# Two-layer decoder trunk: the dense SwiGLU stage with gate and up weights side by side and products of 512 columns

## The reference

```python
def swiglu(h, w_gate, w_up, w_down):
    return (jax.nn.silu(h @ w_gate) * (h @ w_up)) @ w_down

h = rmsnorm(x, ffn_norm[0])                  # 256 x 1024
x = x + swiglu(h, dense_w_gate[0], dense_w_up[0], dense_w_down[0])   # 1024 x 2816, 2816 x 1024
```

## Time and profile before

| what | value |
|---|---|
| time, median of 3 runs | 1540.76 us (1540.14 to 1541.29) |
| time of the profiled execution | 1540.58 us |
| its span | 1538.7 us |
| TensorE busy | 1500.0 us, 97% |
| VectorE busy | 1201.2 us, 78% |
| ScalarE busy | 965.0 us, 63% |
| dense stage, first product to the first instruction behind it | 316.33 to 512.81 us of the span |
| mean granted TensorE clock, share of full | 0.992 |

### The profile page before, as it was taken

One profiled execution on the slowest core, in us unless ns is written; L12 is line 12 of the kernel. 1 busy time (PEld: TensorE's weight loads), 2 busy tenths in 40 slices (PEclk: granted clock), 3 DMA queues, 4 the chain that ended last, 5 costly groups with the idle time before them and its releaser, 6 DMA issues.

```text
span 1538.7 us, 21907 instructions
## 1 busy us (share of the span) xinstructions
PE 1500.0 (97%) x8346; PEld 1286.5 (84%) x8346; DVE 1201.2 (78%) x986; ACT 965.0 (63%) x801; POOL 113.8 (7%) x64
## 2 busy tenths in 40 slices
PE   6999999999999989999999999999999999999996
PEld 6999999889998868888888888888888888888885
DVE  7877677664445678888888888888888888888886
ACT  4444444454343657777777777777777777777775
POOL 1332232100000000000000000000000000000000
PEclk9999999999999999999999999999999999999999
DMA  9644334265456388999999899899899999999980
GB/s 376 211 137 138 138 137 138 85 197 188 169 191 247 137 328 342 378 357 399 353 363 404 341 367 400 349 354 403 347 377 380 359 369 376 364 378 359 395 324 29
DMA packets 66862, 449.40 MB, mean 292 GB/s; under 512 B 7648, under 2 KB 9440, under 8 KB 14448
## 3 DMA queue, kind: packets, MB, share of 16 engines
q1 hardware_dynamic: 63264, 439.84, 74.2%
q0 software_dynamic: 3392, 8.69, 2.2%
q10 hardware_dynamic: 144, 0.02, 0.0%
HBM read 440.65 MB, written 7.86 MB: 291 GB/s over the span
## 4 chain that ended last, share of the span: by engine, by line
PE 93%; DVE 3%; DMA 1%; ACT 1%; issue 1%; SPq 0%; DVEq 0%; ACTq 0%
PE bank L376 29%; PE bank L377 29%; PE bank L378 29%; PE bank L1360 2%; PE bank L1513 2%; DVE w_lo L328 1%; DMA raw<-in_units 1%; PE bank L1347 1%; PE bank L1337 1%; DVE rot L890 1%; PE bank L1522 0%; ACT w_hi L323 0%; PE bank L1380 0%; PE bank L1444 0%; PE bank L1472 0%
## 5 line engine op out<-in xcount | busy, mean ns | idle before, releaser
L328 DVE TENSOR_TENSOR w_lo<-raw,w_hi 128x2048 fp32r<-128x2048 f32 x201 | 460.7, 2294 | 154.7 <-ACT w_hi L323 153.3
L323 ACT ACTIVATE w_hi<-raw 128x2048 fp32r<-128x2048 f32 x201 | 384.7, 1915 | 152.1 <-PE bank L378 140.9
L376 PE MATMUL bank<-w_hi,xg_hi 128*128 128x512 f32 x896 | 359.2, 401 | 0.0
L377 PE MATMUL bank<-w_lo,xg_hi 128*128 128x512 f32 x896 | 354.7, 396 | 0.0
L378 PE MATMUL bank<-w_hi,xg_lo 128*128 128x512 f32 x896 | 354.5, 396 | 0.0
L328 DVE TENSOR_TENSOR w_lo<-raw_late,w_hi 128x2048 fp32r<-128x2048 f32 x95 | 217.8, 2292 | 45.9 <-ACT w_hi L323 44.7
L328 DVE TENSOR_TENSOR w_lo<-raw_more,w_hi 128x2048 fp32r<-128x2048 f32 x96 | 219.8, 2290 | 26.2 <-ACT w_hi L323 25.8
L323 ACT ACTIVATE w_hi<-raw_more 128x2048 fp32r<-128x2048 f32 x96 | 184.6, 1923 | 55.7 <-PE bank L378 55.7
L323 ACT ACTIVATE w_hi<-raw_late 128x2048 fp32r<-128x2048 f32 x95 | 182.2, 1918 | 34.1 <-PE bank L378 34.1
L378 PEld LDWEIGHTS bank<-w_hi,xg_lo 128*128 128x128 f32 x896 | 168.5, 188 | 41.0
L376 PEld LDWEIGHTS bank<-w_hi,xg_hi 128*128 128x128 f32 x896 | 168.7, 188 | 38.7
(11 more groups left out here) (200 smaller groups left out, 1898.5 us busy)
## 6 DMA issues: line engine op xcount, KB each, us to landing
raw<-in_expert_units SPq DMA_DIRECT2D x128, 1024.0 KB, 5.4
raw_more<-in_expert_units SPq DMA_DIRECT2D x96, 1024.0 KB, 5.5
raw_late<-in_expert_units SPq DMA_DIRECT2D x96, 1024.0 KB, 4.9
raw<-in_units SPq DMA_DIRECT2D x73, 1024.0 KB, 4.9
hn<-in_expert_units SPq DMA_DIRECT2D x16, 1024.0 KB, 6.8
qkT<-in_xT SPq DMA_DIRECT2D x2, 512.0 KB, 4.7
raw<-in_units SPq DMA_DIRECT2D x2, 512.0 KB, 7.0
x<-in_x SPq DMA_DIRECT2D x1, 1024.0 KB, 9.2
```

The source lines that it names most:

```text
L323: nc.scalar.activation(w_hi[:, u % SPLIT, :], where, ACT.Copy).then_inc(hi_ready, 1)
L328: nc.vector.tensor_tensor(w_lo[:, u % SPLIT, :], home(u, i)[0], w_hi[:, u % SPLIT, :].bitcast(F32), ALU.subtract).then_inc(lo_ready, 1)
L376: nc.tensor.matmul(bank, hi, w[0], start=start, stop=False)
L377: nc.tensor.matmul(bank, hi, w[1], start=False, stop=False)
```

## The change

The units of a block's gate and up weights are packed in another way, and the list calls them `first` and `second`. `first` holds channels 0 to 511 of both: for each 128 channels, 256 gate columns and beside them 256 up columns. `second` holds channels 512 to 1023 in the same form. A product takes 512 columns, so a unit is 8 products (24 TensorE instructions) and a token tile has a bank of its own, gate values on the left, up values on the right. Both units add to the same banks. Even blocks use banks 4 and 5, odd ones 6 and 7 (`dense_bank`); the turned hidden block goes into the first of the block's own two banks, once `dh` has been made from them. SiLU and `dh` of a block both follow its `second` unit; the turn of block b stands ahead of `second` b + 1 where it stood ahead of gate b + 1. The number of units, their size and the down units stay.

```diff
 for _b in range(N_FB):
-    DENSE_SEQ += [("gate", _b), ("up", _b)]
+    DENSE_SEQ += [("first", _b), ("second", _b)]
...
+        def dense_bank(b, t):
+
+            return ps[4 + 2 * (b % 2) + t][:, :]
...
             for s, (kind, b) in enumerate(DENSE_SEQ):
-                if kind == "up":
+                if s and DENSE_SEQ[s - 1][0] == "second":
+                    d = DENSE_SEQ[s - 1][1]
                     act.wait_ge(unit_used, U_DENSE + s)
-                    if b:
-                        act.wait_ge(dh_ready, b)
+                    if d:
+                        act.wait_ge(dh_ready, d)
                     for t in range(TT):
-                        last = nc.scalar.activation(dsg[:, t, :], ps[4][:, t * FB:(t + 1) * FB], ACT.Silu,
-                                                    scale=rstd(1, t))
+                        last = nc.scalar.activation(dsg[:, t, :], dense_bank(d, t)[:, 0:FB], ACT.Silu, scale=rstd(1, t))
...
-                if (kind == "gate" and b) or s == len(DENSE_SEQ) - 2:
-                    d = b - 1 if kind == "gate" else b + 1
+                if (kind == "second" and b) or s == len(DENSE_SEQ) - 2:
+                    d = b - 1 if kind == "second" else b + 1
                     act.wait_ge(dtr_ready, d + 1)
...
-                        last = nc.vector.scalar_tensor_tensor(dh[:, t, :], ps[5][:, t * FB:(t + 1) * FB], rstd(1, t),
+                        last = nc.vector.scalar_tensor_tensor(dh[:, t, :], dense_bank(d, t)[:, FB:2 * FB], rstd(1, t),
                                                               dsg[:, t, :], ALU.mult, ALU.mult)
...
             def turn_dense_hidden(b):
                 pe.wait_ge(dh_ready, b + 1)
-                if b:
-                    pe.wait_ge(dlo_ready, b)
                 for k in range(2):
                     for t in range(TT):
                         c = k * SEQ + t * P
-                        last = nc.tensor.transpose(ps[6][:, c:c + P], dh[:, t, k * P:(k + 1) * P], ident[:, :])
+                        last = nc.tensor.transpose(dense_bank(b, 0)[:, c:c + P], dh[:, t, k * P:(k + 1) * P], ident[:, :])
...
-                if kind == "gate" and b:
+                if kind == "second" and b:
                     turn_dense_hidden(b - 1)
                 pe.wait_ge(lo_ready, u + 1)
-                if kind == "gate":
-                    if b:
-                        pe.wait_ge(dsilu_ready, b)
-                    full_unit(u, ps[4], None if b else KD + QUARTERS)
-                elif kind == "up":
-                    if b:
-                        pe.wait_ge(dh_ready, b)
-                    full_unit(u, ps[5])
+                if kind != "down":
+                    half = 0 if kind == "first" else 1
+                    for t in range(TT):
+                        for k in range(4):
+                            if b == 0 and t == 0 and k % 2 == 0:
+                                pe.wait_ge(a_lo_ready, KD + QUARTERS + 4 * half + k + 2)
+                            hi, lo = act_of(4 * half + k, t)
+                            last = product(dense_bank(b, t), hi, lo, halves(u, k * 512, 512), half == 0 and k == 0, half == 1 and k == 3)
+                    last.then_inc(unit_used, 1)
...
-                units[u] = block(arrays["dense_w_" + kind][0], 0, D, b * FB, FB)
+                half = 0 if kind == "first" else D // 2
+                both = np.concatenate([arrays["dense_w_" + name][0][half:half + D // 2, b * FB:(b + 1) * FB] for name in ("gate", "up")],
+                                      axis=1)
+                units[u] = block(both, 0, D // 2, 0, 2 * FB)
```

More of the change, by code:

```diff
@@ L613, in _ @@
                     split_hi(act, U_POOL)
-                if (kind == "gate" and b) or s == len(DENSE_SEQ) - 2:
-                    d = b - 1 if kind == "gate" else b + 1
+                if (kind == "second" and b) or s == len(DENSE_SEQ) - 2:
+                    d = b - 1 if kind == "second" else b + 1
                     act.wait_ge(dtr_ready, d + 1)
-                    nc.scalar.activation(dense_hidden_T(d)[0][:, :, :], ps[6][:, :].rearrange("p (k t) -> p k t", k=2), ACT.Copy)\
+                    nc.scalar.activation(dense_hidden_T(d)[0][:, :, :], dense_bank(d, 0).rearrange("p (k t) -> p k t", k=2), ACT.Copy)\
                         .then_inc(dhi_ready, 1)
@@ L937, in _ @@
             for s, (kind, b) in enumerate(DENSE_SEQ):
-                if s and DENSE_SEQ[s - 1][0] == "up":
+                if s and DENSE_SEQ[s - 1][0] == "second":
                     d = DENSE_SEQ[s - 1][1]
@@ L951, in _ @@
                     split_lo(dve, U_POOL)
-                if (kind == "gate" and b) or s == len(DENSE_SEQ) - 2:
-                    d = b - 1 if kind == "gate" else b + 1
+                if (kind == "second" and b) or s == len(DENSE_SEQ) - 2:
+                    d = b - 1 if kind == "second" else b + 1
                     dve.wait_ge(dhi_ready, d + 1)
                     h_hi, h_lo = dense_hidden_T(d)
-                    nc.vector.tensor_tensor(h_lo[:, :, :], ps[6][:, :].rearrange("p (k t) -> p k t", k=2),
+                    nc.vector.tensor_tensor(h_lo[:, :, :], dense_bank(d, 0).rearrange("p (k t) -> p k t", k=2),
                                             h_hi[:, :, :].bitcast(F32), ALU.subtract).then_inc(dlo_ready, 1)
@@ L1281, in project, with full_unit @@
                 last.then_inc(unit_used if q % 4 == 3 else piece_ready, 1)
-            def full_unit(u, bank, before=None):
+            def full_unit(u, bank):
                 for t in range(TT):
                     for k in range(KD):
-                        if before is not None and t == 0 and k % 2 == 0:
-                            pe.wait_ge(a_lo_ready, before + k + 2)
                         hi, lo = act_of(k, t)
```

## The result

The changed kernel takes **1531.05 us** (median of 4 runs, 1530.88 to 1531.11) against 1540.94 us before (4 runs, 1540.14 to 1541.29): a ratio of 0.9934, with a 95% interval of 0.9921 to 0.9947. The profiled execution took 1531.06 us.

The account below looks back on a forecast made before the run. TensorE, busy 97% of the span, was taken to bound the kernel. Wider products 3.5 us plus stalls 1.6 and 1.9 made 7.0 us off, from 1540.6 or the median to 1533.6 or 1533.8; forecast 1533.7 us, range 1532.0 to 1536.5.

Parts of the forecast that it names:

- Direction, and which engine counts: Whole program: TensorE's time is the program's; faster by more than 0.2% with chance 0.90, within 0.07, slower 0.03.
- Stalls: Dense stage, first block and last but one: TensorE's waits for `dh` ahead of the turn vanish, saving 1.6 and 1.9 us.
- the scaling: VectorE's pooling-weight scaling: its load stays as late as ever, but 3.9 us more cover removes TensorE's stall, saving 1.9 us.
- The last block: End of the dense stage: hidden low half ready at 5.8 us, 0.2 left before down 10; cost 0, at most 0.4.
- Hidden halves, banks, loads: Dense stage: halves need 1.7 us of 6.0 between turn and down unit; banks and loads add no waits; cost 0.
- Wider products: Dense gate and up products: 96 of 256 columns become 48 of 512, saving 0.32 us a block, 3.5 us in all.
- The range: Whole program: 1532.0 to 1536.5 us around the forecast of 1533.7 us.
- rival C: Products with `a`: smaller fixed part, half way 0.2367 us apart, saving 1.8 us; 1535.4 us in all, chance 0.03.
- Rival A's wandering clock: Between pooling and experts: sum holds, half-clock stretch may shift by 2 us of work; 1532 to 1535.7 us, chance 0.80.
- B: Dense stage's first block and end: stalls only move; 1535.7 us, or 1537.2 if nothing of them is gained; chance 0.09.
- D: Dense 512-column products: widening brings nothing, only stalls go or they stay too; 1537.2 to 1540.7 us, chance 0.05.
- E: Down units: each waits for the hidden block's low half, 1.0 us lost in ten blocks; slower, 1543.7 us, chance 0.03.

## Why the prediction was wrong

- *Direction, and which engine counts*: right. TensorE takes all of it, and nothing ahead of the stage or behind it changed.
- *Stalls*: right. 1.6 + 1.9 = 3.5 us forecast, 3.19 + 0.26 = 3.45 shown. The chains came out as worked: `dh` of block 0 ready at 330.81 (330.8 forecast), the turn at 332.82 (333.1); the scaling still waits 4.85 us for its load (4.9), and with down 8 starting at 474.6 (485.64 - 5.44 - 5.59) it ends 6.5 us behind that start (6.4), `dh` 7.3 behind (7.3), the turn at 11.0 (11.2).
- *The last block*: right. The low half ends at 497.35, 5.76 us behind the start of down 9 (5.8), and down 10 starts at 497.62: no wait, with 0.27 us left.
- *Hidden halves, banks, loads*: cost 0, as forecast; no wait of TensorE in the stage.
- *Wider products*: wrong, and this is all of the miss. The failing step is "The 512-column row has other operands (`dhT` instead of `a`), but the same types, shapes and weight loads". I took the 0.2333 of the earlier trace rows, measured with a stationary operand that starts 96 bytes past a multiple of 128, for products with `a`, which starts on one. With `a` they are 0.2267: 48 take 11.03 us with their restart where 96 took 11.58 (5.75 + 5.83), 0.55 us a block instead of 0.32, 6.0 instead of 3.5 in eleven blocks. The 0.32 fits neither kind of start (0.55 and 0.02), since its 0.120 came from the one and its 0.2333 from the other.
- *The range*: rival C did ask about the distance with `a`, but bounded it by 0.2333 from below, "between 0.2333, as in the down units, and 2 x 0.120". No reason stood behind that lower bound. The same 0.0067 us allowed on the other side of 0.2333 would have put the low end at 1533.7 - 528 x 0.0067 = 1530.2 and held the result.
- Rival A's wandering clock and rivals B, D and E did not come. The rule of the Trainium skill weighed in the prediction (TensorE: Matmul & The Clock Gate, "Back-to-back issue gap") gives a fixed part of 2.5 ns, and gives it for a product that stands alone; here 2 x 0.120 - 0.2267 = 13.3 ns go with each merged pair, so rows and page are further apart than the prediction had them.

What is open: why the start counts, whether its unit is 64 or 128 bytes, and why 256 columns go the other way. The expectations argued with a bound between a low and a high part of the partition; that was never the cause, and it fitted because every tile that was moved low also came to start on a multiple of 128. That only the start counts is read from all runs together and was not tested by itself. At 512 columns the runs show it for the stationary operand; at 256 both roles of `a` were affected. That the ten or so 512-column products behind a turn are slower (0.231) was seen in each such kernel, and not tested. The Trainium skill (TensorE: Matmul & The Clock Gate, "Step-by-step: what each phase is for") says that the stationary operand has a read port of its own, so that its loading takes nothing from the product that runs. What these runs add is that the start address of what is loaded sets the distance of the products all the same.

## What to carry to other kernels

A duration taken from a row with another operand is a duration with another address: bound it on both sides, however alike types and shapes are. Where TensorE sets the time, look up where the tiles start that are stationary in products of 512 columns, put those that start off a multiple of 128 bytes on one, and measure it; here addresses alone were worth 25 us, two and a half times the change. When two kernels are compared, print the addresses of both: a tile added or resized in one of them moves the others. And price a stall by its row, but remember that the clock may fall behind it.

## What was unexpected of the hardware

- 512 columns, full clock: 0.2267 us apart with a stationary operand that starts on a multiple of 128 bytes, low or high in the partition, 0.2333 with one that starts 96 bytes past it. 4032 expert products make 22.7 us of it.
- 256 columns: 0.120 us with `a` on a multiple of 128 bytes, 0.117 with `a` 96 bytes past it. There two narrow products cost as much as one wide one (11.29 and 11.27 us a block).
- A wait of 1.68 us left the clock at 1.00 in one kernel; waits of 1.90 and 2.15 us in two others were followed by some 3 us at 1.2 GHz.
